# A search for best keys beside the compression of keys, and a sample group's last stages beside the experts' gathers

## The chip, the cores and the metric

One core of one Trainium2 chip runs the whole program. The metric is the device time of one execution in microseconds (us), lower is better. Three timed runs of the kernel before and one profiled execution are shown. PE is TensorE, DVE is VectorE, ACT is ScalarE, POOL is GpSimd, SP is SyncE, which here only issues DMAs.

## The reference

One layer of a decoder, for a prompt group (1 x 512 tokens, width 1024) and a sample group (8 sequences, one new token each, 4096 past tokens in paged caches of 128 rows). Both share all weights.

```python
xn = rmsnorm(x); p = xn @ w_in                       # one projection, columns split among the heads
# A: an indexer scores all keys, the best 256 are gathered, attention over them
# B: keys compressed by an MLP over strided chunks; the best 16 blocks of 64 tokens, gathered;
#    a window of 512; the three summed with gates
# M: attention into 256 memory tokens
u = einsum('btcw,cwd->btcd', stack([o_a, o_b, o_m]), w_branch)
h = x + sum(sigmoid(xn @ w_gate) * u, axis=2) @ w_out
q = rmsnorm(h) @ w_pq                                # 8 heads, each scored against 2 x 128 sub-keys
v_top, i_top = top_k(scores, 16); f_v, f_p = top_k(v_top[0] + v_top[1], 16)
g = softmax(f_v); e = the 16 experts of 16384
a = gelu(einsum('nhkd,nd->nhk', u_tab[e], xf))
y = h + einsum('nhk,nhkd->nd', g * a, v_tab[e])
```

For the sample group the compression reads all 256 pages of `cache_cmp_kv` (128 KB each), the search takes the best 256 of 4097 scores of each sample, and each of the 8 tokens draws 128 experts.

## The kernel before

Everything is float32. The program first projects, then does the prompt's attention, then the experts; the samples' attention lies beside the prompt's experts.

**The loop of gathers.** `mix_prompt` (line 3215) goes through 512 slots, 4 tiles of 128 tokens times 128 experts of each token. Slot n is one indirect DMA issued by POOL (line 3256): 128 rows of 8 KB, u and v of the expert side by side, into one of 7 buffers (`NBUF`). DVE multiplies u with the token's row and sums (line 3288), ACT makes the coefficient (gelu, times gate; lines 3316 and 3318). Three steps later (`LAG`) coefficient times v is added to y: either by DVE (line 3283), or by PE as a product with a diagonal matrix that ACT makes (lines 3323 and 3350). `adds_on_vector` says which; before, PE has steps 0 to 61, 175 to 238 and those of `SELECT`, DVE the rest. POOL issues slot s once slot s - 7 is summed and so free.

**Lanes beside the loop.** Each engine's program is in order. Work beside the loop is written as stages, each for a number of steps (`self.block(steps)`), and an engine's part yields fractions of its stage: `Beside.advance` puts the instructions up to step s ahead of the loop's instructions of step s. So a stage that waits on an engine holds the loop's instructions behind it. A stage begins, on every engine, with a wait until the lane's stage before has ended on all its engines. There are two lanes, `beside` and `aside`. SP has no part in the loop: it works through its own parts of the stages, in the order of steps but without being held to the loop's pace.

**Stages in order** (first step to last): retrieval of the prompt's later heads and tile 0 to 61; merge of gates, products, norm, products of the prompt's second half 62 to 174; retrieval of its tiles 175 to 238; weights of the compression 239 to 244; compression 245 to 316; index scores 317 to 344; queries 345; search for the best keys (`select_keys`) 346 to 381, with the window's attention and the memory's on the other lane from 348 and 354 on; attention over compressed keys 382 to 395; rows of the found keys 396 to 428; attention over them to 447; gather of chosen blocks 448 to 456; attention over blocks 457 to 496. The loop ends at step 519, after slot 511.

**Compression** (`compress_samples`, line 1253): 16 chunks of 16 pages, 3 buffers. For each page SP loads its number from a table and issues its DMA; chunk n is issued once PE has done chunk n - 3 (`part_mm`). PE does a chunk with 32 matmuls (line 1337), two chunks make a sample.

**Search** (`select_keys`, line 2294): 128 partitions hold 16 segments of each sample's scores. DVE does 32 rounds of max, max_index, match_replace (lines 2398 to 2400), then four levels of merging whose halves SP moves between partitions, then two short products.

**After the loop**, alone on the chip: `finish` calls `finish_rows` with `ahead=True` for the samples (merge of the branches, w_out, norm, w_pq; both weights are loaded during the merge), then `expert_samples`: the scores of 8 tokens, top 16, eight gathers of 1 MB, eight dot products, 32 matmuls, the store.

Of the kernel before, what the change touches and what calls it, by code (L numbers as in the profile page):

```python
# [8 lines left out]
F32 = mybir.dt.float32  # L9
U32 = mybir.dt.uint32  # L10
I32 = mybir.dt.int32
# [69 lines left out]
WEIGHTS, COMPRESS, INDEX, SELECT = 6, 72, 28, 36  # L81
WINDOW_FROM, WIN_AT, MEMORY, CMP_AT, DSA_AT, SEL_AT = 348, 16, 70, 14, 18, 40
DSA_ROWS = 30
# [144 lines left out]
class Kernel:  # L228
# [398 lines left out]
    def build(self):  # L627
        nc, i, o = self.nc, self.i, self.o
        with self.ctx:
# [17 lines left out]
            self.finish()  # L647
# [605 lines left out]
    def compress_samples(self, wts):  # L1253

        nc, i, ident = self.nc, self.i, self.ident
        tag = "cs"
# [3 lines left out]
        tmp = ExitStack()  # L1260
        with tmp:
            w2 = self.sb("cs_w2", [P, P], F32, tmp)
            table = self.sb("cs_table", [1, DB * NPAGE], I32, tmp)
            ch = self.sb("cs_ch", [P, NBUF, NPAGE // 2, 2, PAIRS, KV, 8], F32, tmp)
            part = self.sb("cs_part", [P, 2, 2, KV, NCH_S], F32, tmp)
# [5 lines left out]
            hp = self.ps("cs_hp", [P, 2, 512], tmp)  # L1271
            op = self.ps("cs_op", [P, 2, KV, 2, DH], tmp)
            kt = self.ps("cs_kt", [P, 512], tmp)
            (weights_in, table_in, zeroed, chain, part_mm, part_act, part_dve, hid_mm, hid_done, out_mm, out_v, kn_done, root_done, sq_sum,
             kt_mm, kt_out) = (self.sem(f"cs_{n}") for n in (
                 "weights_in", "table_in", "zeroed", "chain", "part_mm", "part_act", "part_dve", "hid_mm", "hid_done", "out_mm", "out_v",
# [9 lines left out]
            with self.block(WEIGHTS) as block:  # L1286
                @block.vector
                def _(dve):
                    dve.memset(w2[:], 0.0).then_inc(zeroed, 1)

                @block.sync
                def _(sp):
                    sp.dma_start(table[:], bass.AP(i["page_table"].tensor, 0, [[0, 1], [1, DB * NPAGE]])).then_inc(table_in, 16)
                    for c in range(2):
                        for j in range(2):
# [2277 lines left out]
```

## Time and profile before

| | |
|---|---|
| three runs, median | 2792.5 us (2788.6 to 2797.1) |
| the profiled execution | 2781.6 us, its span 2779.9 us |
| PE / DVE / ACT / POOL busy | 65% / 63% / 24% / 31% of the span |
| granted PE clock, mean | 0.787 of full |
| DMA | 727.7 MB, mean 262 GB/s; the gathers' queue 577 MB |

The chain that ended last names only the last 2% of the span, so the profile has to be read by stages: busy time of each engine, PE clock and DMA share in the stretch of each stage, and in it who waits for whom. "DMA share" is the mean busy share of the sixteen DMA engines.

### The profile page before, as it was taken

What the parts mean: (1) busy time and instruction counts of PE and PEld (TensorE: products, weight loads), DVE (VectorE), ACT (ScalarE), POOL (GpSimd) and SP (SyncE); (2) the same over time, 40 slices, a digit from 0 to 9 for tenths busy, and PEclk for the clock granted to TensorE, in tenths of its full rate; (3) what the DMA queues carried; (4) which work ended last, traced back from release to release, by engine and by line L of the source; (5) the groups of instructions that cost most, each with busy time, mean ns of one, the idle gap of its engine ahead of it and who ended that gap; (6) DMA issues with size and microseconds to landing.
All of it is one profiled execution on the core that took longest, in us unless ns stands there. A gap on an engine that the chain in (4) does not pass through costs nothing. (4 is left out here: it accounts for less than half of the span.)

```text
span 2779.9 us, 25050 instructions
## 1 busy us (share of the span) xinstructions
PE 1812.3 (65%) x6605; PEld 1000.1 (36%) x6605; DVE 1761.6 (63%) x3916; ACT 670.4 (24%) x2035; POOL 864.9 (31%) x829
## 2 busy tenths in 40 slices
PE   7999799699836738844467515665877533418374
PEld 3466476444412213312222114444743213304311
DVE  3343465711168967685789965666779688859813
ACT  2011266410113323321233211222222111214100
POOL 1000042200024723342353432221531477654301
PEclk9999799899969969977799957878568755555586
DMA  4122320043248989997998898996986799899863
GB/s 150 25 88 76 96 92 2 1 166 130 104 167 349 421 348 358 355 392 306 377 379 326 356 367 311 350 355 246 404 343 247 295 351 374 324 363 398 330 227 122
DMA packets 200920, 727.69 MB, mean 262 GB/s; under 512 B 39785, under 2 KB 83330, under 8 KB 133898
## 3 DMA queue, kind: packets, MB, share of 16 engines
q0 software_dynamic: 84384, 577.16, 52.0%
q1 hardware_dynamic: 115226, 144.70, 15.3%
q10 hardware_dynamic: 1168, 4.23, 0.4%
q8 instruction: 54, 0.88, 0.1%
q14 instruction: 88, 0.72, 0.1%
HBM read 717.42 MB, written 12.66 MB: 263 GB/s over the span
## 5 line engine op out<-in xcount | busy, mean ns | idle before, releaser
L3256 POOL DMA_INDIRECT ex_pairs<-in_uv_tab,e_idx x147 | 196.0, 1333 | 552.9 <-POOLq L3153 246.7
L3316 ACT ACTIVATE ex_coef<-ex_dots 128x1 f32<-128x1 f32 x512 | 103.6, 202 | 1046.8 <-DVE ex_dots L3288 953.9
L3256 POOL DMA_INDIRECT branch_rows_t<-in_uv_tab,e_idx x163 | 192.2, 1179 | 256.8 <-DVE heads_t L3283 160.4
L3256 POOL DMA_INDIRECT heads_t<-in_uv_tab,e_idx x146 | 186.0, 1274 | 268.4 <-DVE heads_t L3283 146.8
L1337 PE MATMUL cs_pp<-cs_ch,xn_t 128*128 128x256 f32 x512 | 146.3, 456 | 175.9 <-DMA cs_ch<-in_cache_cmp_kv 175.9
L3288 DVE CUSTOM_DVE_ANT_0 branch_rows_t<-branch_rows_t,heads_t 128x1024 f32<-128x1024 f32 x163 | 198.6, 1220 | 55.2 <-DMA branch_rows_t<-in_uv_tab,e_idx 50.3
L3288 DVE CUSTOM_DVE_ANT_0 ex_pairs<-ex_pairs,heads_t 128x1024 f32<-128x1024 f32 x147 | 179.5, 1222 | 60.9 <-DMA ex_pairs<-in_uv_tab,e_idx 58.9
L820 PE MATMUL in_acc<-in_w,xn_t 128*128 128x512 f32 (+7 forms) x560 | 208.1, 527 | 5.8 <-POOLq L178 4.0
L3288 DVE CUSTOM_DVE_ANT_0 heads_t<-heads_t 128x1024 f32<-128x1024 f32 x146 | 178.1, 1221 | 37.8 <-DMA heads_t<-in_uv_tab,e_idx 34.9
L1337 PEld LDWEIGHTS cs_pp<-cs_ch,xn_t 128*128 128x128 f32 x512 | 118.5, 235 | 205.9 <-DMA cs_ch<-in_cache_cmp_kv 106.8
L3283 DVE SCALAR_TENSOR_TENSOR heads_t<-branch_rows_t,ex_coef,heads_t 128x1024 f32<-128x1024 f32 x118 | 151.2, 1281 | 30.6 <-issue 14.7
L3318 ACT ACTIVATE ex_coef<-ex_coef,e_gate 128x1 f32<-128x1 f32 x512 | 150.8, 295 | 16.6
L3350 PE MATMUL ex_y_ps<-ex_pairs,heads_t 128*128 128x512 f32 x188 | 98.9, 657 | 76.9 <-ACT heads_t L3323 71.8
L3283 DVE SCALAR_TENSOR_TENSOR heads_t<-ex_pairs,ex_coef,heads_t 128x1024 f32<-128x1024 f32 x100 | 127.9, 1279 | 28.5 <-issue 24.9
L3283 DVE SCALAR_TENSOR_TENSOR heads_t<-heads_t,ex_coef 128x1024 f32<-128x1024 f32 x100 | 128.0, 1280 | 25.5 <-issue 22.2
L820 PEld LDWEIGHTS in_acc<-in_w,xn_t 128*128 128x128 f32 (+1 forms) x560 | 95.1, 174 | 108.3 <-issue 88.4
L3350 PE MATMUL ex_y_ps<-heads_t 128*128 128x512 f32 x184 | 99.0, 667 | 47.8 <-ACT heads_t L3323 38.6
L3350 PE MATMUL ex_y_ps<-branch_rows_t,heads_t 128*128 128x512 f32 x180 | 96.2, 666 | 31.8 <-ACT heads_t L3323 30.9
L1638 PE MATMUL at_t_ps<-at_diag,at_exp 128*128 128x128 f32 (+3 forms) x608 | 87.6, 288 | 21.7 <-POOL at_diag L1726 20.9
L2925 PE MATMUL fq_mg_g_ps<-fq_mg_wg,xn_t 128*128 128x512 f32 x192 | 85.0, 596 | 0.0
L3350 PEld LDWEIGHTS ex_y_ps<-ex_pairs,heads_t 128*128 128x128 f32 x188 | 35.6, 205 | 135.5 <-ACT heads_t L3323 97.8
L1638 PEld LDWEIGHTS at_t_ps<-at_diag,at_exp 128*128 128x128 f32 (+3 forms) x608 | 71.9, 185 | 34.6 <-POOL at_diag L1726 22.0
(727 smaller groups left out, 3435.1 us busy)
## 6 DMA issues: line engine op xcount, KB each, us to landing
cs_ch<-in_cache_cmp_kv SPq DMA_DIRECT2D x256, 128.0 KB
fq_mg_wg<-in_w_gate SPq DMA_DIRECT2D x6, 2048.0 KB
in_w<-in_w_in SPq DMA_DIRECT2D x4, 2048.0 KB, 11.3
first_w<-in_w_gate SPq DMA_DIRECT2D x3, 2048.0 KB, 7.9
fp_wb<-in_w_branch SPq DMA_DIRECT2D x6, 1024.0 KB, 10.2
fp_wg<-in_w_gate SPq DMA_DIRECT2D x3, 2048.0 KB, 8.1
fq_mg_wb<-in_w_branch SPq DMA_DIRECT2D x6, 1024.0 KB
fs_mg_wb<-in_w_branch SPq DMA_DIRECT2D x6, 1024.0 KB, 9.8
```

Of the source, the lines that this page charges most:

```text
L820: last = pe.matmul(acc[:r, u % 2, :n], self.xT[:, k, P * t:P * t + r], w[:, j % 2, k, :n], start=(k == 0), stop=(k == KD - 1))
L1337: last = pe.matmul(pp[:, n % 2, 256 * c:256 * c + 256].rearrange("p (g k m) -> p g k m", g=KV, m=8), wts[:, c, r, :], ch[:, n % NBUF, :, c ...
L1638: last = pe.matmul(t_ps[:w, u % 2, k, :], ex[:, u % 6, P * k:P * k + w], diag[:, u % 4, :], start=True, stop=True)
L2925: last = pe.matmul(g_ps[:r, u % 2, :], xT[:, k, cols], wg[j % depth][:, k, :], start=(k == 0), stop=(k == KD - 1))
L3256: pool.indirect_dma_start(out=pair(s), out_offset=None, in_=i["uv_tab"], in_offset=bass.IndirectOffsetOnAxis(ap=idx[:, t, m:m + 1], axis=0 ...
L3283: dve.scalar_tensor_tensor(out=y(t), in0=v(n), scalar=coef[:, t, m:m + 1], in1=y(t), op0=ALU.mult, op1=ALU.add).then_inc(acc_done, 1)
L3288: dve.tensor_tensor_reduce(out=u(s), in0=u(s), in1=x(t), scale=1.0, scalar=0.0, op0=ALU.mult, op1=ALU.add, accum_out=dots[:, t, m:m + 1]). ...
L3316: act.activation(c, dots[:, t, m:m + 1], ACT.Gelu_apprx_tanh).then_inc(gelu_done, 1)
L3318: act.activation(c, c, ACT.Copy, scale=gate[:, t, m:m + 1]).then_inc(coef_done, 1)
L3350: last = pe.matmul(y_ps[:, q, :], diag[:, (pe_upto[n] - 1) % NDIAG], v(n)[:, 512 * q:512 * q + 512], start=n in first_pe, stop=n in last_pe)
```

## The change

The search for best keys moves to the second lane and runs beside the compression, which now stands behind the index scores; the compression's weights are loaded in one step ahead of the index. The samples' merge, products, norm and experts become stages beside the gathers, at the end of the lane; w_out and w_pq are now loaded by their own stages. The loop's sums from step 267 on alternate, even slots on DVE and odd ones on PE. New steps: weights 239, index 240 to 267, compression 268 to 339, beside it the search 268 to 317, the picks 318 to 333, their places 334 to 336; queries 340; window 341 to 362 and memory 363 to 422 on the second lane; compressed keys' attention 341 to 354, found rows 341 to 370, attention over them to 389, gather of blocks 390 to 397, attention over blocks 399 to 442; merge 443 to 452, turn, w_out 456 to 465, norm, w_pq 472 to 481, turn, experts of the samples 485 to 519. Some buffers change place (the window's values, the search's lists, two banks of PSUM become one).

```diff
-WEIGHTS, COMPRESS, INDEX, SELECT = 6, 72, 28, 36
-WINDOW_FROM, WIN_AT, MEMORY, CMP_AT, DSA_AT, SEL_AT = 348, 16, 70, 14, 18, 40
+INDEX, COMPRESS, SELECT, PICKED = 28, 72, 50, 16
+WIN_AT, MEMORY, CMP_AT, DSA_ROWS, DSA_AT, SEL_AT = 16, 60, 14, 30, 18, 44
+LAST_MERGE, LAST_TURN, LAST_LINEAR, LAST_NORM, LAST_ROWS = 10, 3, 10, 6, 34
+GATHERED, MIXED = 10, 28
...
-    picking = retrieving + RETRIEVE_LAST + WEIGHTS + COMPRESS + INDEX
-    return not (step < RETRIEVE_HALF + RETRIEVE_NEXT or retrieving <= step < retrieving + RETRIEVE_LAST or picking <= step < picking + SELECT)
+    indexing = retrieving + RETRIEVE_LAST
+    if step < RETRIEVE_HALF + RETRIEVE_NEXT or retrieving <= step < indexing:
+        return False
+    return step < indexing + INDEX or m % 2 == 0
...
             with self.block(COMPRESS) as block:
                 @block.sync
                 def _(sp):
+                    sp.wait_ge(table_in, 16)
                     for n in range(2 * DB):
                         if n >= NBUF:
+                            yield at((n - NBUF) // 2, 0.1 + 0.5 * ((n - NBUF) % 2))
                             sp.wait_ge(part_mm, n - NBUF + 1)
...
-                        if u >= 2:
-                            pe.wait_ge(hid_done, u - 1)
+                        if u:
+                            pe.wait_ge(hid_done, u)
...
     def sample_attention(self):
...
+                weights = self.sample_compress_weights(tmp, wts)
+                self.index_scores()
+                self.recycle()
+                indexed = main.before
+                self.aside.next_step = main.next_step
+                self.compress_samples(tmp, wts, weights, part)
+                self.beside = self.aside
+                with ExitStack() as sk:
+                    chosen = self.select_keys(sk, [(main.ended, indexed)])
+                    self.aside.next_step += PICKED
+                    self.place_keys(chosen, phys, past_ix, is_new)
...
             with self.block(SELECT) as block:
                 @block.sync
                 def _(sp):
+                    for sem, value in ready:
+                        sp.wait_ge(sem, value)
                     sp.dma_start(work[:, :W], bass.AP(s["score"].tensor, 0, [[W, NSEG], [PAST, DB], [1, W]])).then_inc(work_in, 16)
...
                         for n in range(LEVELS):
                             half = P >> (n + 1)
+                            yield 0.61 + 0.2 * n / LEVELS
                             sp.wait_ge(merged, n + 1)
...
+            work = ExitStack()
+            with work:
+                self.finish(work, keys)
...
-            with nc.Block() as block:
+            remembered = self.aside.ended, self.aside.before
+            with self.block(LAST_MERGE) as block:
                 @block.sync
                 def _(sp):
-                    sp.dma_start(gate8[:], self.s["gate8"].rearrange("j b n -> b j n")).then_inc(gate_in, 16)
                     for j, (q, c) in enumerate(jobs):
                         sp.dma_start(wb[:, j], i["w_branch"][c, :, 512 * q:512 * q + 512].rearrange("(k p) n -> p k n", p=P)).then_inc(w_in[j], 16)
                     for dst, src in also:
                         sp.dma_start(dst, src).then_inc(also_done, 16)
-                    for dst, src, loaded in ahead:
-                        sp.dma_start(dst, src).then_inc(loaded, 16)
+                    sp.wait_ge(*remembered)
+                    sp.dma_start(gate8, self.s["gate8"].rearrange("j b n -> b j n")).then_inc(gate_in, 16)
...
             @block.sync
             def _(sp):
-                beside.advance("sync", sp, 10 ** 9)
+                for s in list(range(end)) + [10 ** 9]:
+                    beside.advance("sync", sp, s)
+                    aside.advance("sync", sp, s)
...
+            with self.block(LAST_ROWS) as block:
                 @block.gpsimd
                 def _(pool):
                     pool.memset(q[:], 0.0).then_inc(zeroed, 1)
-                    pool.wait_ge(idx_done, 2)
                     for n in range(N):
-                        pool.indirect_dma_start(out=pairs[:, n], out_offset=None, in_=i["uv_tab"],
+                        yield at(GATHERED + 0.8 * n)
+                        if n == 0:
+                            pool.wait_ge(idx_done, 2)
+                        pool.indirect_dma_start(out=pairs[n], out_offset=None, in_=i["uv_tab"],
```

## Rows read from the trace of the kernel before

**Rows 1.** The page's slices of the span, 40 of 69.5 us each
```profile
DMA  4122320043248989997998898996986799899863
GB/s 150 25 88 76 96 92 2 1 166 130 104 167 349 421 348 358 355 392 306 377 379 326 356 367 311 350 355 246 404 343 247 295 351 374 324 363 398 330 227 122
```

**Rows 2.** Timeline of DVE; start, duration, line; steps 239 and 511
```profile
1599.55 1.22 DVE L3288 CUSTOM_DVE_ANT_0 ex_pairs<-ex_pairs,heads_t 128x1024 f32<-128x1024 f32 x1
...
2632.85 1.23 DVE L3288 CUSTOM_DVE_ANT_0 ex_pairs<-ex_pairs,heads_t 128x1024 f32<-128x1024 f32 x1
```

**Rows 3.** Busy us by stage: stretch, length, PE, PEld, DVE, ACT, POOL, clock, DMA, GB/s
```profile
1600.00:1613.00 13.00, 0.00 (x0) 0.00 (x0) 12.95 (x19) 2.88 (x12) 6.77 (x6) 0.50 1.11 354
1613.00:1956.00 343.00, 177.00 (x676) 137.70 (x676) 208.18 (x365) 67.15 (x195) 97.01 (x79) 0.74 0.88 326
1956.00:2052.00 96.00, 83.32 (x373) 78.19 (x373) 84.52 (x150) 22.34 (x74) 42.26 (x36) 0.52 0.92 376
2052.00:2214.00 162.00, 108.27 (x286) 46.48 (x286) 119.27 (x349) 35.04 (x111) 47.96 (x53) 0.84 0.73 287
2214.00:2374.00 160.00, 47.29 (x183) 35.84 (x183) 129.93 (x212) 30.07 (x103) 121.07 (x108) 0.53 0.95 367
2374.00:2488.00 114.00, 33.19 (x128) 22.80 (x127) 71.33 (x104) 20.48 (x76) 67.80 (x58) 0.50 0.84 328
2488.00:2600.00 112.00, 95.75 (x336) 60.03 (x336) 103.09 (x139) 38.21 (x148) 49.65 (x40) 0.50 0.97 391
2600.00:2634.00 34.00, 0.00 (x0) 0.00 (x0) 33.89 (x45) 6.97 (x28) 12.38 (x11) 0.50 0.92 367
2634.00:2780.00 146.00, 80.10 (x204) 22.09 (x204) 37.73 (x89) 10.90 (x27) 9.88 (x9) 0.75 0.45 167
...
805.00:2634.00 1829.00, 1045.43 (x3131) 575.39 (x3131) 1389.97 (x2748) 462.50 (x1435) 767.93 (x629) 0.73 0.89 349
```

**Rows 4.** Waits in the compression: total us, times, longest
```profile
PE cs_pp L1337 <- DMA cs_ch<-in_cache_cmp_kv: 175.9, 15, 76.5
```

**Rows 5.** Timeline of SP: start, us, issues; pages 0 to 47, then 48 to 255
```profile
1609.90 72.38 SPq L1314 DMA_DIRECT2D cs_ch<-in_cache_cmp_kv  x48
...
1683.08 238.84 SPq L1314 DMA_DIRECT2D cs_ch<-in_cache_cmp_kv  x208
```

**Rows 6.** Timeline of PE: two chunks that follow each other
```profile
1801.86 8.58 PE L1337 MATMUL cs_pp<-cs_ch,xn_t 128*128 128x256 f32 x32 [6.54 <-DMA cs_ch<-in_cache_cmp_kv]
...
1817.74 9.17 PE L1337 MATMUL cs_pp<-cs_ch,xn_t 128*128 128x256 f32 x32 [6.41 <-DMA cs_ch<-in_cache_cmp_kv]
```

**Rows 7.** Timeline of SP: the scores stored, then loaded for the search
```profile
2045.86 0.39 SPq L2211 DMA_DIRECT2D tmp_score<-is_score  x1
2051.83 0.61 SPq L2342 DMA_DIRECT2D sk_work<-tmp_score  x1
```

**Rows 8.** Groups of DVE in the search, 2052 to 2214: busy us, mean ns, idle before
```profile
L2398 DVE MAX8 sk_best<-sk_work 128x8 f32<-128x257 f32 x32 | 13.6, 425 | 0.4
L2399 DVE FIND_INDEX8 sk_ix<-sk_best,sk_work 128x8 uint32<-128x257 f32 x32 | 13.4, 420 | 0.0
L2400 DVE MATCH_REPLACE8 sk_work<-sk_best,sk_work 128x257 f32<-128x257 f32 x32 | 13.2, 412 | 0.0
```

**Rows 9.** The page's group of sums on DVE: busy us, mean ns, idle before
```profile
L3283 DVE SCALAR_TENSOR_TENSOR heads_t<-branch_rows_t,ex_coef,heads_t 128x1024 f32<-128x1024 f32 x118 | 151.2, 1281 | 30.6 <-issue 14.7
```

**Rows 10.** Timeline of PE: one sum, its four matmuls, in the index stage
```profile
2043.82 3.58 PE L3350 MATMUL ex_y_ps<-branch_rows_t,heads_t 128*128 128x512 f32 x4 [0.26 <-issue]
```

**Rows 11.** Largest group of PE at 1406 to 1600
```profile
L3350 PE MATMUL ex_y_ps<-branch_rows_t,heads_t 128*128 128x512 f32 x79 | 39.6, 629 | 11.1 <-ACT heads_t L3323 10.9 <-issue 0.2
```

**Rows 12.** Timeline of the tail: first gather, its first use, the last matmuls
```profile
2735.15 0.95 POOL L3403 DMA_INDIRECT es_pairs<-in_uv_tab,es_idx  x1 [16.73 <-DVE es_idx L3483]
...
2740.98 1.23 DVE L3492 CUSTOM_DVE_ANT_0 es_pairs<-es_pairs,es_xf 128x1024 f32<-128x1024 f32 x1 [4.62 <-DMA es_pairs<-in_uv_tab,es_idx]
...
2760.99 15.32 PE L3422 MATMUL es_y_ps<-es_pairs,es_diag 128*8 128x512 f32 x32 [32.59 <-ACT es_diag L3438]
```

More of the change, by code:

```diff
@@ new lines, in sample_dsa @@
+            prob = self.sb("cm_prob", [DB * HQ, NCH_S + DB], F32, ctx)
+            compressed = self.beside.ended, self.beside.before
+            queries = self.spread_queries(qz, qa, placed)
+            compared = []
+            windowed = self.sample_window(ctx, qz, nsa, queries, compressed, compared)
+            self.sample_memory(bank, queries)
+            rows_at = self.beside.next_step
+            landed = self.gather("da_rows", [(kv[:, n // DB, n % DB, :], i["cache_a_kv"].rearrange("n p w -> (n p) w"), phys[:, n:n + 1]) for n in range(2 * DB)]
+                                 + [(bias[:, n // DB, n % DB, :], s["bias_pos"], past_ix[:, n:n + 1]) for n in range(2 * DB)], apart=True, steps=DSA_ROWS,
+                                 behind=placed)
@@ new lines, in sample_dsa @@
+            self.attend_samples("cm_at", NCMP_S, HQ, qz, keys=lambda b: self.kc_t[:, b, :NCMP_S],
+                                values=lambda b, j: self.vc[:min(P, NCMP_S - P * j), b, j].rearrange("p g d -> p (g d)"), acc=nsa, turned=False,
+                                waits=lambda b: [queries], bias=self.bias_cmp, prob=prob, gate=self.gate_bh[:, 0:1], add=False, steps=CMP_AT, scoring=0.3)
+            compared.append((self.beside.ended, self.beside.before))
+            self.pick_blocks(prob, sl_rows, sl_bias_rows)
@@ L2456, in select_keys @@
             rows = s["cand"].rearrange("p (k w) -> (p k) w", w=1)
-            picked = self.gather("sk_pick", [(t_f[:, n:n + 1], rows, cand_at[:, n:n + 1]) for n in range(NC)], apart=True, steps=16)
+            picked = self.gather("sk_pick", [(t_f[:, n:n + 1], rows, cand_at[:, n:n + 1]) for n in range(NC)], apart=True, steps=PICKED)
             return picked, t_f, t_i, page, hot
@@ L2727, in finish_rows @@
             out_w = pq_w = None
-            loads = []
-            if ahead:
-                out_w, pq_w = ((self.sb(f"{tag}_{n}_early", [P, 2, KD, 512], F32, tmp)[:], [self.sem(f"{tag}_{n}_early{b}") for b in range(2)])
-                               for n in ("out", "pq"))
-                loads = [(w[:, b], i[name][:, 512 * b:512 * b + 512].rearrange("(k p) n -> p k n", p=P), sems[b])
-                         for name, (w, sems) in (("w_out", out_w), ("w_pq", pq_w)) for b in range(2)]
             weights, after, then = None, [], []
@@ L2767, in finish_rows @@
             turn("mixed", t_view, load_h)
-            self.linear(f"{tag}_out", t_view, rows, i["w_out"], D, h, add=h, loaded=out_w, ahead=then)
-            if not ahead and not early:
+            self.linear(f"{tag}_out", t_view, rows, i["w_out"], D, h, add=h, loaded=out_w, ahead=then, steps=linear_steps)
+            if not early:
                 self.recycle()
-            self.norm_rows(f"{tag}_ffn", h, i["ln_ffn"], rows, t_view, keep=xf)
-            self.linear(f"{tag}_pq", t_view, rows, i["w_pq"], D, mixed, also=[(save, h)] if save is not None else (), loaded=pq_w)
+            self.norm_rows(f"{tag}_ffn", h, i["ln_ffn"], rows, t_view, keep=xf, steps=norm_steps)
+            self.linear(f"{tag}_pq", t_view, rows, i["w_pq"], D, mixed, also=[(save, h)] if save is not None else (), loaded=pq_w, steps=linear_steps)
             turn("pq", x_t)
```

309 lines of the change are left out of this document (168 added, 141 removed).

## The prediction

> **What bounds the kernel now.** I read the page first: its slices [rows 1] show that from about 800 us on the sixteen DMA engines are eight to nine tenths busy, and that the last slices fall off. That is the loop of 512 gathers (1 MB each, one a step). Its first dot product starts at 812 us; the n-th execution of line 3288 on VectorE is step n, and with that the stages can be laid on the clock: step 239 is at 1599.6 us and step 511, the last, at 2632.9 us [rows 2]. Then I read one window per stage [rows 3]. The reader is to see three kinds. In most of them the DMA share is 0.92 to 0.97 (there the transfers are the limit, 367 to 391 GB/s). In two it is lower though all engines have room: the compression (343 us for 72 steps, 4.8 us a step, share 0.88) and the search for best keys (162 us for 36 steps, share 0.73). And the last 146 us, where the samples' own merge, products, retrieval and experts run alone, have a share of 0.45, 66 us of DMA work in 146.
>
> Inside the compression, TensorE waits 175.9 us in 15 waits for the pages of the cache [rows 4]. Pages are issued by SP, one instruction chain each: 208 of them take 238.8 us without a hole, 1.15 us a page or 18.4 us for the 16 pages of one chunk [rows 5], and TensorE starts chunks 16 to 18 us apart, though one takes it 8.6 to 9.2 us [rows 6]. So SP's issuing sets the pace of that stage.
>
> **A rule weighed.** The Trainium skill ("DMA: Bandwidth & Descriptors", Issuing engines are not separate DMA queues) says that the sequencer's time to start a DMA is usually small beside the transfer. By that rule the stage would be priced by its bytes. The trace doesn't agree: 208 issues stand back to back over 238.8 us while TensorE waits [rows 4, 5]; what the rule would make of the time is the first rival.
>
> **The change, part by part**, each step range with its time before and after. Steps 0 to 238 are not touched: 1599.6 us stay.
>
> Index (steps 239 to 267): the weights' stage shrinks from 6 steps to 1, index keeps 28. Before, 28 steps took about 96 us [rows 3]; with one more step 100 us.
>
> Compression with the search beside it (steps 268 to 339). Both start at once, and SP serves both in the order of steps: it first issues 48 pages, and only then the table of scores that VectorE's search needs at step 271. 48 pages took 72 us when the gathers competed [rows 5]; at 1.15 us each 55. VectorE, and with it the gathers, stands still meanwhile; I take 58 us, near the undisturbed rate since the gathers stop too, and 6 us more for the scores to land (the hand-over of the same data took 6 us from store to next load [rows 7]). That is a new wait, and behind it on VectorE stand all dot products. Then some 18 us until TensorE has done chunk 0 and SP may issue the fourth. The other 208 pages take 239 us. The search's own DMAs on SP hold pages back: four exchanges of lists and two round trips for the bar; the trace has no such wait beside pages, so from 0 (TensorE's three chunks of stock cover it) to six times 6 us; I take 12. After its last page the stage took 35 us more (1921.9 to 1956). Sum 58 + 6 + 18 + 239 + 12 + 35 = 368, say 370 us (330 to 400), for 343 before. The search on VectorE costs 13.6 + 13.4 + 13.2 us in its three large groups [rows 8], 40 us, and some 70 (an estimate) with the levels of merging behind them; VectorE was busy 208 of 343 us [rows 3] and gives 36 sums of 1.28 us [rows 9] to TensorE, so 208 - 46 + 70 = 232 us of 370: hidden, until VectorE's idle time, some 140 us, is gone. What was 162 us of its own for the search is gone.
>
> Steps 340 to 370 (window, compressed keys' attention, picked blocks, gathers of rows): 47 such steps took 160 us [rows 3], 3.4 a step, so 31 take 105; the window's 4.2 MB, which lay in the search before, add 11 at 367 GB/s: 116 us (105 to 130).
>
> Steps 371 to 398 (the attention over chosen keys, gather of blocks): 28 steps took 114 us; 3 us more for memory rows: 117.
>
> Steps 399 to 442 (attention over blocks): 2.8 us a step [rows 3], 44 steps 123 us, and 3.4 MB of memory rows 9: 132 us. Here the alternation weighs: a sum on TensorE, four matmuls, took 3.6 us at the lower level of its clock [rows 10] and 2.0 us (79 matmuls in 39.6 us) in a stage where sums filled it [rows 11]; and TensorE was already busy 95.8 of 112 us with the clock at 0.50. 22 sums more are 44 to 79 us, on 96 x 44/40 = 105 us: 149 us at the cheaper price of a sum and 184 at the dearer; the attention's own matmuls would also take about half if the clock rose for them, which would leave the 123 us of the gathers as the limit. I take 145 (123 to 184), near the first of these, since the clock was 0.84 in the one stage where sums and attention shared TensorE (2052 to 2214).
>
> The Trainium skill ("TensorE: Matmul & The Clock Gate", What's actually happening) has the clock released by activity. The trace only half agrees: 0.84 at 108 of 162 us busy, but 0.50 at 96 of 112 [rows 3]. By the page this part would cost 132; I don't rely on it.
>
> Samples' finish beside gathers (steps 443 to 510). Bytes: 68 gathers are 71 MB, the weights 6.3 + 4.2 + 4.2, the samples' eight gathers 8.4, gain and small 0.5: 95 MB. At the best window's 391 GB/s 243 us, at the 328 of the stretch with most hand-overs (2374 to 2488) 290. The chain now loads w_out and w_pq in their own stages (they were loaded ahead), so TensorE waits for them with sums queued behind it; POOL, up to seven gathers ahead, waits at step 485 for the turned rows and at 495 for the indices, and one gather needs 5.8 us from issue to the first use [rows 12]. I take 265 us, midway. VectorE's and TensorE's own work of the tail (38 and 80 us [rows 3]) is spread over it.
>
> End (from step 511): seven steps of sums, the eight diagonals, 32 matmuls in 15.3 us [rows 12], the addition and store, 7 + 2 + 15 + 3 = 27 us (to 40), in place of the 147 us from 2632.9 to 2779.9.
>
> **Sum.** 100 + 370 + 116 + 117 + 145 + 265 + 27 = 1140 us in place of 1180; the execution ends at 1599.6 + 1140 = 2739.6, and with the 1.7 us that lie between span 2779.9 and time 2781.6 that is 2741. The median of the runs, 2792.5, is 10.9 above the profiled one, which makes 2752, rounded: I forecast **2750 us** as median, 1.5% faster. A cross-check: DMA busy time from step 239 on is the sum of share times length over rows 3, 976 us; the forecast gives it 1113 us outside the end, a share of 0.88, which is what the loop has now (0.89).
>
> **Rivals.** First, SP's issuing is no limit and the freed VectorE lets the gathers run at 0.95, the share of the better windows: 976 / 0.95 = 1027, plus 27 is 1054 in place of 1140, so about 2665 us. For it speaks that the tail is idle at 0.45 and that VectorE loses 110 us of work (122 sums on TensorE from step 267 on in place of 36, 86 x 1.28); against it the unbroken issues [rows 5]. This is also what the page named above would give.
>
> Second, slower: **TensorE becomes the bound at half clock**. With sums on every second step it has gaps and stays at 1.2 GHz: 3.6 us every two steps. Attention over blocks goes to 184 (+39); the finish, where TensorE has the tail's 80 us of matmuls [rows 3] at the mixed clock of 0.75 and 34 sums of 3.6, gets +25, as a chain through slower matmuls (80 x 0.75 / 0.5 = 120, +40, of which part is covered); the compression +10: 2750 + 74 = 2824. It decides once work per step on TensorE, 2.4 us of attention and 1.8 of sums, passes the 2.8 us of a gather. For it: a clock of 0.50 to 0.53 in all windows from 2214 to 2634. Against: 0.84 where every sum ran on TensorE.
>
> Third, no change: the first wait of the search costs the full 72 us and the finish comes at 290: 2750 + 14 + 12 for SP's exchanges + 25 = 2801 at most, 2790 typical; the tail's gain is spent on new waits.
>
> **Chances.** Forecast 0.56 (2690 to 2780), first rival 0.21, second 0.12, third 0.11. A measurement can tell about 0.3% from none, 8 us: faster than 2784 holds the forecast and the first rival, 0.77; within 0.11; slower 0.12. The range 2665 to 2805 leaves out the faster half of the first rival and most of the second.
>
> **What would show it.** After: dot product 268 near 1700 us, then a hole of 50 to 70 us in them with SP issuing 48 pages; step 340 near 2070; TensorE's waits for pages still near 150 us; no stretch with only the search; sums on TensorE in every second step, at a clock of 0.6 to 0.8; last dot product near 2710; end 27 us later. The prediction is wrong if the compression with the search takes under 330 or over 400 us, if the finish takes over 4.3 us a step, or if attention over blocks takes over 4 us a step with TensorE full.

## The result, and the profile after

The kernel after takes 2808.9 us (median of 11 runs, 2799.0 to 2820.9), the kernel before in the same comparison 2786.9 us (11 runs, 2780.5 to 2797.2). The ratio is 1.0076 with a 95% interval of 1.0054 to 1.0098: **slower by 0.8%**, where 2750 us and faster was forecast, and above the top of the range, 2805. The profiled execution of after took 2820.9 us (the highest of its runs), its span is 2817.5 us. It moves 727.66 MB, before 727.69.

The page's slices, to be laid beside [rows 1] (40 of 70.4 us each; DMA is the busy share in tenths, GB/s what was moved):

```profile
DMA  4122310054158989897998797796869898887776
GB/s 148 25 93 71 115 69 2 1 180 163 53 230 355 400 339 373 347 395 303 363 376 331 271 416 268 280 368 234 299 244 376 346 370 342 315 315 275 305 320 254
```

Most of the drop in before's last slices (227 and 122 GB/s) is gone, as intended. In its place stand 268 and 280 from 1690 us on, 234 and 244 between 1900 and 2110, and nothing above 320 in the last six slices. The windows by stage (stretch, length, busy us of PE, PEld, DVE, ACT and POOL with instructions, granted clock, DMA share, GB/s), beside [rows 3]:

```profile
1606.00:1624.00 18.00, 3.65 (x16) 3.28 (x16) 3.16 (x7) 1.08 (x3) 10.37 (x10) 0.50 0.96 274
1624.00:1722.00 98.00, 85.26 (x380) 77.31 (x380) 83.76 (x146) 22.34 (x74) 44.21 (x42) 0.53 0.91 368
1722.00:1778.00 56.00, 3.78 (x4) 1.18 (x4) 7.89 (x14) 1.89 (x7) 3.03 (x3) 0.54 0.63 221
1778.00:1886.00 108.00, 83.68 (x291) 53.11 (x292) 103.62 (x267) 28.03 (x85) 32.05 (x29) 0.86 0.95 355
1886.00:2006.00 120.00, 70.81 (x239) 44.89 (x238) 61.92 (x167) 22.20 (x63) 20.79 (x20) 0.72 0.70 246
...
2344.00:2503.00 159.00, 147.24 (x532) 90.48 (x533) 87.32 (x130) 47.71 (x178) 52.93 (x46) 0.74 0.82 311
2503.00:2556.00 53.00, 39.59 (x77) 9.03 (x76) 24.07 (x35) 6.98 (x25) 12.30 (x11) 0.86 0.87 321
2556.00:2696.00 140.00, 72.72 (x175) 25.96 (x175) 62.59 (x93) 26.99 (x90) 37.42 (x34) 0.75 0.76 295
2696.00:2792.00 96.00, 45.16 (x64) 14.75 (x62) 62.48 (x119) 22.31 (x72) 31.80 (x31) 0.66 0.89 367
2792.00:2818.00 26.00, 17.97 (x37) 3.97 (x36) 7.62 (x13) 2.75 (x12) 0.00 (x0) 0.83 0.06 22
805.00:2792.00 1987.00, 1267.70 (x3639) 629.82 (x3639) 1318.38 (x2736) 504.19 (x1536) 742.14 (x638) 0.78 0.86 333
```

Four stretches are to be seen. At 1722 to 1778 (steps 268 to 270) and 1886 to 2006 (steps 300 to 317) no engine is full (at most 71 of 120 us in the second) and the DMA share is 0.63 and 0.70: somebody waits. At 2344 to 2503 (attention over blocks) PE is busy 147 of 159 us: it is the bound. At 2556 to 2696 (from the samples' turn and w_out on) the share is 0.76 and again no engine is full.

With the n-th dot product as the mark of step n, as in the prediction, the miss in the profiled execution, 77.9 us on 2739.6, falls into these parts. It is larger than the 59 us by which the medians miss, since this execution is 12 us above the median of its kernel, and the profiled one of before was below its own:

| steps | forecast us | after us | miss |
|---|---|---|---|
| start to 239 | 1599.6 | 1606.1 | +6.5 |
| 239 to 268, index | 100 | 116.3 | +16.3 |
| 268 to 340, compression and search | 370 | 384.2 | +14.2 |
| 340 to 371 | 116 | 121.0 | +5.0 |
| 371 to 399 | 117 | 116.4 | -0.6 |
| 399 to 443, attention over blocks | 145 | 158.8 | +13.8 |
| 443 to 511, samples' finish | 265 | 289.4 | +24.4 |
| end | 27 | 25.2 | -1.8 |

Steps 0 to 238 run the same work; their 6.5 us are the spread of executions (1593 to 1609 in the kernels below). Part of the 14.2 us is spread too: four kernels below with the same code in steps 268 to 339 (e4, e7, e8, e12) take 369.0 to 378.3 us for them.

**The waits of the search.** SP's timeline (start, us, line, what, count) at step 268, and the wait of DVE at step 270:

```profile
1716.92 55.30 SPq L1319 DMA_DIRECT2D cs_ch<-in_cache_cmp_kv  x48
1772.26 0.60 SPq L2367 DMA_DIRECT2D sk_work<-tmp_score  x1
```
```profile
DVE sk_best L2429 <- DMA sk_work<-new_key_score: 45.3, 1, 45.3
```

It is the forecast hole: 48 pages before the table of scores, 1.15 us a page. SP's timeline from there to the end of its pages, and DVE's waits in 1886 to 2006:

```profile
1791.78 109.80 SPq L1319 DMA_DIRECT2D cs_ch<-in_cache_cmp_kv  x96
1901.62 0.55 SPq L2376 DMA_DIRECT2D sk_moved<-sk_best  x1
...
1903.57 17.21 SPq L1319 DMA_DIRECT2D cs_ch<-in_cache_cmp_kv  x16
1920.82 8.17 SPq L2376 DMA_DIRECT2D sk_moved<-sk_over  x2
1929.79 16.81 SPq L1319 DMA_DIRECT2D cs_ch<-in_cache_cmp_kv  x16
1946.65 0.73 SPq L2376 DMA_DIRECT2D sk_moved<-sk_over  x1
1958.30 17.24 SPq L1319 DMA_DIRECT2D cs_ch<-in_cache_cmp_kv  x16
1975.59 0.37 SPq L2382 DMA_DIRECT2D tmp_bar<-sk_bar  x1
1978.46 0.62 SPq L2384 DMA_DIRECT2D sk_bar<-tmp_bar  x1
1980.48 93.56 SPq L1319 DMA_DIRECT2D cs_ch<-in_cache_cmp_kv  x64
```
```profile
DVE sk_over L2458 <- DMA sk_bar<-tmp_bar: 16.8, 1, 16.8
DVE sk_over L2441 <- DMA sk_moved<-sk_best: 16.7, 1, 16.7
...
DVE sk_over L2441 <- DMA sk_moved<-sk_over: 12.9, 2, 10.8
```

An exchange of lists that DVE needs at once stands in SP's order behind pages that nobody needs yet, the first behind the end of a run of 96, later ones behind a chunk of 16, 17 us. DVE waits 46.4 us for them, and behind it on DVE stand all dot products. I had looked at it from the other side only: what the exchanges do to the pages. TensorE waited for pages 11.7 us and not some 150 (the page's group of its matmuls; idle before in the last column):

```profile
L1344 PE MATMUL cs_pp<-cs_ch,xn_t 128*128 128x256 f32 x512 | 118.1, 390 | 11.7 <-DMA cs_ch<-in_cache_cmp_kv 11.7
```

**The waits of the finish**, 2503 to 2792 us (total, times, longest):

```profile
PE fs_pq_acc L488 <- DMA fs_pq_w<-in_w_pq: 21.5, 1, 21.5
DVE fs_mixed L3038 <- DMA xn_t<-tmp_gate: 21.1, 1, 21.1
...
PE fs_out_acc L488 <- DMA fs_out_w<-in_w_out: 18.6, 1, 18.6
```

PE waits in full for each of the two weights that were loaded ahead before, and the merge for its gates, whose load stands on SP behind the 6 MB of w_branch: these took SP 24.5 us to issue (2502.27 to 2526.78), the gates' load followed at 2529.17, and the merge could begin at 2539.7.

### The profile page after: what moved, and what is told of

It reads as the page before. It is cut to its first block and busy times, and to the rows that moved or that the text cites. A ratio compares the mean times of both kernels' runs of the same rounds, so it can differ in the third digit from the quotient of the medians.

```text
span 2817.5 us, 25696 instructions
## 1 busy us (share of the span) xinstructions
PE 1972.8 (70%) x6945; PEld 1035.6 (37%) x6945; DVE 1660.0 (59%) x3831; ACT 703.6 (25%) x2121; POOL 828.7 (29%) x829
## 2 busy tenths in 40 slices
DMA packets 200778, 727.66 MB, mean 258 GB/s; under 512 B 39769, under 2 KB 83186, under 8 KB 133754
## 5 line engine op out<-in xcount | busy, mean ns | idle before, releaser
L3382 PE MATMUL ex_y_ps<-branch_rows_t,heads_t 128*128 128x512 f32 x324 | 196.1, 739 | 144.9 <-ACT heads_t L3355 129.6
L3382 PE MATMUL ex_y_ps<-ex_pairs,heads_t 128*128 128x512 f32 x288 | 171.4, 728 | 93.2 <-ACT heads_t L3355 91.7
L3382 PE MATMUL ex_y_ps<-heads_t 128*128 128x512 f32 x280 | 160.7, 705 | 55.3 <-ACT heads_t L3355 54.8
L3382 PEld LDWEIGHTS ex_y_ps<-branch_rows_t,heads_t 128*128 128x128 f32 x324 | 67.5, 227 | 241.3 <-ACT heads_t L3355 149.0
L3382 PEld LDWEIGHTS ex_y_ps<-ex_pairs,heads_t 128*128 128x128 f32 x288 | 60.5, 228 | 183.7 <-ACT heads_t L3355 124.7
L1344 PE MATMUL cs_pp<-cs_ch,xn_t 128*128 128x256 f32 x512 | 118.1, 390 | 11.7 <-DMA cs_ch<-in_cache_cmp_kv 11.7
L3315 DVE SCALAR_TENSOR_TENSOR heads_t<-branch_rows_t,ex_coef,heads_t 128x1024 f32<-128x1024 f32 x82 | 105.0, 1281 | 28.1 <-issue 16.6
L3315 DVE SCALAR_TENSOR_TENSOR heads_t<-ex_pairs,ex_coef,heads_t 128x1024 f32<-128x1024 f32 x75 | 96.0, 1280 | 26.9 <-issue 24.1
L3382 PEld LDWEIGHTS ex_y_ps<-heads_t 128*128 128x128 f32 x280 | 55.6, 215 | 140.1 <-ACT heads_t L3355 87.8
L3315 DVE SCALAR_TENSOR_TENSOR heads_t<-heads_t,ex_coef 128x1024 f32<-128x1024 f32 x76 | 97.3, 1280 | 11.0 <-DMA fs_ffn_gain<-in_ln_ffn 4.0
## 6 DMA issues: line engine op xcount, KB each, us to landing
in_w<-in_w_in SPq DMA_DIRECT2D x4, 2048.0 KB, 11.3
fs_mg_wb<-in_w_branch SPq DMA_DIRECT2D x6, 1024.0 KB, 25.2
```

The source lines that it names most:

```text
L1344: last = pe.matmul(pp[:, n % 2, 256 * c:256 * c + 256].rearrange("p (g k m) -> p g k m", g=KV, m=8), wts[:, c, r, :], ch[:, n % NBUF, :, c ...
L3315: dve.scalar_tensor_tensor(out=y(t), in0=v(n), scalar=coef[:, t, m:m + 1], in1=y(t), op0=ALU.mult, op1=ALU.add).then_inc(acc_done, 1)
L3382: last = pe.matmul(y_ps[:, q, :], diag[:, (pe_upto[n] - 1) % NDIAG], v(n)[:, 512 * q:512 * q + 512], start=n in first_pe, stop=n in last_pe)
```

## The experiments

The ratios are to the kernel before, in parentheses the 95% interval, with the median of the changed kernel. Every kernel is the one after with the edit shown, unless it says otherwise; each computes the whole output. The theory: waits in SP's order of issue and late weights cost the time (A). The rival: sums on PE do (B). Others are named in the expectations.

**e1: Sums back on DVE.**

```diff
-    return step < indexing + INDEX or m % 2 == 0
+    return True
```

> The changed kernel with all sums from step 267 on made by VectorE again (only the alternation is undone). Theory A (the loss sits in waits on SP's queue: 55 us at step 271 and about 46 us at the exchanges of the search) expects little: attention over blocks falls from 159 to some 130 us as TensorE, busy 147 of 159, is relieved, the compression with the search grows by some 15 as VectorE takes 36 sums of 1.28 us back: 2790 to 2805 us for 2809. Rival B (TensorE is the bound of the late stages through its sums) expects 30 us less in attention over blocks and 20 to 30 in the samples' finish: 2750 to 2760 us.

Measured 1.0103 (1.0068 to 1.0138), 2820.7 us: far from B's 2750 to 2760, and above A's 2790 to 2805 too. That it is slower than after (1.0076) the intervals do not tell. The rows of steps 399 to 442 and of 271 to 299:

```profile
2371.00:2507.00 136.00, 119.80 (x448) 83.90 (x448) 112.00 (x152) 39.83 (x156) 54.33 (x47) 0.50 0.95 368
1780.00:1906.00 126.00, 42.42 (x172) 29.82 (x172) 121.46 (x282) 22.71 (x72) 33.91 (x29) 0.65 0.92 319
```

Attention over blocks falls from 158.8 to 135.8 us and is bound by the transfers again (share 0.95 for 0.82). But in the rounds of the search DVE is now full, 121 of 126 us, and steps 271 to 299 take 127 for 108. The finish takes 297.4 us for 289.4. The alternation helps in one place and costs in another; as the cause of the whole, B falls.

**e2: Scores ahead of the pages.** SP loads the table of scores before the first 48 pages.

```diff
                     sp.wait_ge(table_in, 16)
+                    yield 0.02
                     for n in range(2 * DB):
```

> The changed kernel, but SP loads the table of scores for the search ahead of the first 48 pages instead of behind them. Theory A: the hole of 55 us before dot product 271 falls to about 12, and most of it is time won, as the pages were not late afterwards (TensorE waited 12 us for them in all): 2765 to 2775 us. Rival D (SP's issuing of 256 pages, 1.15 us each, sets the length of the stage whatever stands still in it) expects the time back as waits for pages: 2800 to 2810 us.

Measured 1.0063 (1.0036 to 1.0089), 2806.6 us: from 1.0076 no difference that can be told. A had expected 2765 to 2775, D 2800 to 2810. The hole did go: steps 268 to 270 take 10.2 us for 55.2. But SP still has to issue the same pages, now 144 of them in 177 us without a hole, and TensorE waits for them, 42.7 us for 11.7. Steps 271 to 299 take 28 us more and 300 to 317 take 12 more. SP's first run of pages, and TensorE's wait in 1720 to 2100:

```profile
1710.58 177.03 SPq L1320 DMA_DIRECT2D cs_ch<-in_cache_cmp_kv  x144
...
PE cs_pp L1345 <- DMA cs_ch<-in_cache_cmp_kv: 42.7, 5, 17.9
```

Of 45 us, 40 were spent again by step 318. The hole had given SP a head start; without it SP's rate of issue shows. (Over all of steps 268 to 339 the profiled execution takes 365.7 us, 18.5 less than after but only 3 to 13 less than the four kernels with unchanged code there, and the medians lie 2.3 us apart: what stays of it is not told by these runs.)

**e3: Pages apart.** SP issues pages one by one as the steps go, so that an exchange finds a place between them.

```diff
                         for k in range(NPAGE // 2):
+                            if n >= NBUF:
+                                yield at((n - NBUF) // 2, 0.1 + 0.5 * ((n - NBUF) % 2) + 0.03 * k)
```

> The changed kernel, but SP's pages of one chunk are spread over the four steps of that chunk in its order of work, so that the search's exchanges of lists and its bar don't stand behind 16 pages (17 us) each. Theory A: VectorE's waits of 16.7, 12.9 and 16.8 us at the exchanges fall to some 3 each, and 30 to 40 us are won: 2770 to 2780 us. Rival D: pages then wait behind the search instead, TensorE's waits for pages grow by the same: 2800 to 2815 us.

Measured 1.0017 (0.9992 to 1.0043), 2794.1 us: 0.6% faster than after. Steps 300 to 317 take 95.3 us for 119.8 (117.0 to 119.8 in the kernels with unchanged code there), and that is all of the gain up to step 340. SP's timeline in them, and their window:

```profile
1896.33 13.55 SPq L1321 DMA_DIRECT2D cs_ch<-in_cache_cmp_kv  x13
1909.93 0.53 SPq L2378 DMA_DIRECT2D sk_moved<-sk_over  x1
1911.58 8.05 SPq L1321 DMA_DIRECT2D cs_ch<-in_cache_cmp_kv  x8
1921.71 0.74 SPq L2378 DMA_DIRECT2D sk_moved<-sk_over  x1
```
```profile
1875.00:1970.00 95.00, 67.72 (x238) 43.11 (x237) 61.40 (x166) 21.92 (x61) 20.55 (x21) 0.82 0.84 294
```

The work in the window is the same (DVE 61 us in both), the waits behind 16 pages are not there: DVE waits 3.0 us for the later exchanges and 2.7 for the bar, where it waited 12.9 and 16.8. D had expected TensorE's wait for pages to grow, and it stayed at 11.3 us. So A is shown for these. The wait at step 300, for the first exchange, stays (14.2 us for 16.7).

**e5: Both orders together.**

> Both edits of SP's order at once: scores loaded ahead of the pages, and pages spread over their chunk's steps. The scores first gave 4 us and the spread pages 16 us (ratios 1.0063 and 1.0017 for 1.0076). If SP's queue is one resource, the hole at step 271 is paid back only because pages come late later; with the exchanges out of the way too, the two add up at most: ratio 1.000 to before (theory A). If both only shift the same wait, the ratio stays at 1.0017 (rival D).

Measured 0.9992 (0.9966 to 1.0017), 2787.9 us: 0.84% under after, where the two alone gave 0.13 and 0.59%. Whether the first edit adds anything once the second is in these runs don't tell: 0.25% lies between e3 and e5, as much as either interval reaches to one side. In the profiled execution the first hole is gone again (10.4 us for steps 268 to 270), and DVE's wait for the first exchange has grown to 26.7 us.

**e4: The finish alone at the end again**, with everything else as after: the call of `finish` moves behind the loop.

> The changed kernel with the samples' merge, products, retrieval and experts after the loop again, all else as changed (w_out and w_pq are not loaded ahead). Theory A: beside the gathers they take 290 us for 68 steps and 25 at the end; alone the 68 steps are bare at 2.5 us, 170 us, and the tail takes the 147 of before and some 25 more for weights that are not loaded ahead: 342 for 315, so 2830 to 2840 us. Rival C (hand-overs between lanes eat what the overlap gives): 2800 us or less.

Measured 1.0150 (1.0119 to 1.0180), 2830.1 us. In A's range. Steps 443 to 510 take 172.3 us and the end 164.9, together 337.2; after, 289.4 + 25.2 = 314.6. So the finish beside the gathers is a gain of 0.7% even with its waits. And the rest of the change is a loss, in two places. With the finish alone, dot product 511 comes at 2653 us and not at 2633, though the search's own stage is gone: the window and the memory, which lay beside that search [rows 3, 2052 to 2214], now lie beside later steps, and the compression with the search takes 369 us here for 72 steps where before it took 343 alone. And the end takes 165 us where before, with w_out and w_pq loaded ahead, it took 147.

**e6: The kernel before with the alternation** from the search on (all even slots on DVE, odd on PE; nothing else changed).

```diff
+    if step >= picking:
+        return m % 2 == 0
```

> The kernel before with only the alternation: from the search on, even slots' sums on VectorE and odd ones' on TensorE (in the search TensorE had all, later VectorE all; the compression keeps VectorE). In the changed kernel undoing the alternation cost 0.3%, a gain of 34 us elsewhere and a loss of 23 us in attention over blocks. The kernel before has no samples' finish beside the gathers, where it could gain: I expect 20 us lost in attention over blocks and 10 won in the search: ratio 1.000 to 1.005. A ratio under 0.997 would say that the alternation is a gain by itself.

Measured 1.017 (1.011 to 1.023), 2832.6 us. The stage of the search takes 180.8 us for 155.1 (DVE had no sums there before; now it has half of them), attention over blocks 128.9 for 111.7:

```profile
2511.00:2640.00 129.00, 119.79 (x411) 71.43 (x412) 79.12 (x118) 45.06 (x168) 41.69 (x39) 0.76 0.85 333
```

I had expected 10 us won in the search, and 26 were lost. In the order of before, alternating is a loss of its own, 1.7%; 9 us of it lie in steps 245 to 316, which the edit does not touch (352.0 us for 342.7), and stay unexplained. Which engine has room depends on what lies beside the step.

**e8: Alternation everywhere but in the attention over blocks.**

```diff
-    return step < indexing + INDEX or m % 2 == 0
+    return step < indexing + INDEX or 399 <= step < 443 or m % 2 == 0
```

> The changed kernel with sums on VectorE in steps 399 to 442 alone, the alternation kept elsewhere. With all sums on VectorE these steps took 136 us for 159. If TensorE (147 us busy of 159) is the bound there, 20 to 23 us are won: ratio 1.000 (rival B, for these steps alone). If it only moves waits, ratio 1.005 to 1.008.

Measured 0.9983 (0.9952 to 1.0013), 2786.5 us, 0.9% under after. The stage takes 135.8 us for 158.8:

```profile
2335.00:2471.00 136.00, 121.58 (x450) 84.73 (x451) 112.29 (x152) 40.36 (x157) 54.95 (x47) 0.50 0.96 368
```

Here B is right: with 82 matmuls fewer the transfers bound the stage again. What the sums cost on TensorE, from its groups in 2344 to 2503 of after, and the memory's products in 2335 to 2471 of e8 (busy us, mean ns, idle before):

```profile
L3382 PE MATMUL ex_y_ps<-branch_rows_t,heads_t 128*128 128x512 f32 x36 | 26.7, 882 | 0.3 <-issue 0.3
L3382 PE MATMUL ex_y_ps<-heads_t 128*128 128x512 f32 x24 | 16.8, 837 | 0.3 <-issue 0.3
L3382 PE MATMUL ex_y_ps<-ex_pairs,heads_t 128*128 128x512 f32 x24 | 16.3, 815 | 1.2 <-ACT heads_t L3355 1.2
...
L2721 PE MATMUL me_ps<-values,xn_t 128*128 128x1 f32 x112 | 25.0, 353 | 0.0
```

84 matmuls are 21 sums in 59.8 us, 2.85 us a sum. The rest of TensorE's 147.2 us, 87 us, is attention with the memory's products, which took 119.5 us in e8 at the lower level of the clock.

**e7: The finish's weights ahead.** Three of the four halves of w_out and w_pq go into the merge's buffers as its products leave them, during the merge, and the fourth behind w_out's products; the norm gets scratch that is free by then.

```diff
+                loads = [(2, places[0], half("w_out", 0), sems[0]), (4, places[1], half("w_out", 1), sems[1]), (6, places[2], half("w_pq", 0), sems[2])]
+                then = [(nt, places[0], half("w_pq", 1), sems[3])]
...
                     sp.dma_start(gate8, self.s["gate8"].rearrange("j b n -> b j n")).then_inc(gate_in, 16)
+                    for count, dst, src, loaded in loads:
+                        sp.wait_ge(branch_mm, count)
+                        sp.dma_start(dst, src).then_inc(loaded, 16)
```

> The changed kernel, but w_out and w_pq are loaded into the merge's own buffers as these come free, ahead of their stages. TensorE waited 19 and 22 us for them, with odd sums queued behind it, and each of these two stages took 51 us for 10 steps where 10 bare steps take 25. If the waits are the cause (theory A), each falls to about 36 us: 25 to 30 us won, ratio 0.998. If the stages are limited by their bytes, 14.7 MB in 51 us being 288 GB/s (rival E), under 8 us are won: ratio 1.005.

Measured 0.9962 (0.9935 to 0.9988), 2774.5 us, 1.1% under after and now faster than before. The two stages take 33.3 us for 51.7 and 28.4 for 50.8; steps 443 to 510 take 255.0 for 289.4. The bytes are the same, and TensorE's two waits for weights are gone (the merge still waits 21.8 us for its gates); the window over both stages (2530 to 2628) against 0.76 and 295 GB/s in after:

```profile
2530.00:2628.00 98.00, 68.98 (x148) 21.87 (x146) 62.51 (x89) 26.45 (x88) 34.05 (x31) 0.80 0.95 380
```

**e10: All four edits together.**

> The four edits that each won something, together: scores loaded first, pages spread, w_out and w_pq loaded ahead, sums on VectorE in steps 399 to 442. They lie in different steps (268 to 339, 456 to 481, 399 to 442), so theory A and B together expect the gains to add: 0.84 + 1.14 + 0.93 = 2.9% under the changed kernel's 1.0076, ratio 0.979, about 2730 us. If the transfers of the whole loop are the real limit (rival E), the gains overlap and the ratio stays at 0.99.

Measured 0.9772 (0.9737 to 0.9807), **2724.5 us** (six runs, 2716.2 to 2732.8): 2.3% faster than before, 3.0% faster than after. The parts alone (e5, e8, e7) sum to 0.84 + 0.93 + 1.14 = 2.9%: they add up, so they were separate costs. Its loop, to be read beside the last window row of after (0.86, 333 GB/s) and of [rows 3] (0.89, 349):

```profile
805.00:2700.00 1895.00, 1251.30 (x3550) 635.52 (x3551) 1343.22 (x2758) 495.23 (x1513) 745.65 (x637) 0.76 0.89 349
```

**e11: The same with all sums of steps 268 to 317 on PE.**

```diff
+    if 268 <= step < 318:
+        return False
```

> The same with all sums of steps 268 to 317 on TensorE, as the kernel before had them beside its search. Alternating them in the kernel before made its 36 steps of search 26 us longer, as VectorE has search, dot products and sums. Beside the compression TensorE has the chunks too (118 us busy for them). If VectorE is the bound there: 10 to 20 us less than e10_all; if TensorE with pages is: 10 us more.

Measured 0.9784 (0.9740 to 0.9828), 2725.2 us: no difference. Neither the 10 to 20 us less nor the 10 more of the expectation came. In 1717 to 2070 DVE is busy 207 of 353 us, TensorE 262, and the DMA share is 0.85 (0.84 in the same stage of e10). With the orders mended, neither engine bounds the compression. What is left is SP: in e10 issuing its 256 pages takes it 315 us beside a stage of 355. That is an account from the timeline; no run made the issuing itself cheaper.

**e12: The compression's weights on the second lane**, to see whether SP's issues make the 18 us of step 239.

```diff
-                weights = self.sample_compress_weights(tmp, wts)
+                self.beside, self.aside.next_step = self.aside, main.next_step
+                weights = self.sample_compress_weights(tmp, wts, (main.ended, main.before))
+                self.beside = main
+                main.next_step += 1
...
```

> The changed kernel with the compression's weights loaded in a stage of the second lane, so that the index scores don't wait until SP has issued their seven DMAs. Step 239 took 18 us for some 3; if the seven issues (5.5 us) stand in it, it takes 12 us or less. If the hole is POOL's (it goes up to seven gathers ahead and waits for the stage's begin, then the first four index gathers stand ahead of the next dot product's), it stays at 15 to 18.

One execution, 2822.1 us; step 239 takes 22.7 us, neither the 12 of one account nor the 15 to 18 of the other. The start of the index stage in after:

```profile
1610.41 0.94 POOL L2244 DMA_INDIRECT is_ch<-in_cache_a_kidx,chunk_rows  x1 [30.17 <-SPq L180]
...
1613.96 1.28 DVE L3315 SCALAR_TENSOR_TENSOR heads_t<-branch_rows_t,ex_coef,heads_t 128x1024 f32<-128x1024 f32 x1 [3.13 <-DMA is_w<-tmp_w]
...
1616.37 0.94 POOL L3288 DMA_INDIRECT heads_t<-in_uv_tab,e_idx  x1 [0.30 <-issue]
...
1624.14 1.22 DVE L3320 CUSTOM_DVE_ANT_0 heads_t<-heads_t 128x1024 f32<-128x1024 f32 x1 [8.89 <-DMA heads_t<-in_uv_tab,e_idx]
```

In before (first two lines) and in e12 (last line):

```profile
1943.34 0.94 POOL L2221 DMA_INDIRECT is_ch<-in_cache_a_kidx,chunk_rows  x1 [31.68 <-DVEq L177]
...
1948.31 0.94 POOL L3256 DMA_INDIRECT heads_t<-in_uv_tab,e_idx  x1 [0.30 <-issue]
...
1625.15 1.28 DVE L3320 SCALAR_TENSOR_TENSOR heads_t<-branch_rows_t,ex_coef,heads_t 128x1024 f32<-128x1024 f32 x1 [19.78 <-DMA is_w<-tmp_w]
```

POOL reaches the start of the index stage seven gathers ahead and stands there 24 to 32 us, until the stage before has ended; then it issues the index's own gathers, and only 5 to 6 us later one of the loop. In after DVE's 18.0 us between dot products 239 and 240 hold three waits: 2.9 us until SP has issued the seven loads, 3.1 for `is_w`, the index scores' weights, whose load follows on SP, and 8.9 for the loop's gather. In e12 POOL was released 6 us earlier against the loop's steps and issued the loop's next gather at 1607.33, but DVE stood 19.8 us for `is_w` (by the profile), still issued behind the seven loads. So the edit moved a wait and took none away, and what each of the three costs alone stays open. The kernel before has such a hole too: its dot product 316 is at 1934.8 us and 317 at 1956.5. I had read "28 steps in 96 us" from a window that begins at 1956.

## Why the prediction was wrong, point by point

**What bounds it.** The reading of before held: SP's issuing sets the compression's pace (in e2, once the hole is gone, 144 pages are issued in 177 us without a pause while TensorE waits for them), the tail left the DMA engines idle, and attention over blocks is bound by transfers as long as PE has no sums (135.8 us in four kernels, 132 worked out). The list of stretches with a low share left out one of its own rows, 2374 to 2488 with 0.84, but the sums used it.

**Index, 100 for 116.** A term taken from a window that starts behind the hole at the stage's first step. A hole of this kind came along with the stage: step 239 alone takes 18.0 us.

**Compression and search, 370 for 384.** The first hole was right: 55.2 us for steps 268 to 270. Wrong was the next term, 12 us for SP's exchanges: I priced the wait of the pages for the exchanges (6 us each at most, hidden by three chunks), and put the wait of DVE for an exchange behind pages at nothing; it was 46 us in sum. Since pages are issued 1.15 us apart [rows 5], 16 of them are 18 us, and each DMA in the same order can wait that long; the rows for it were there. Followed along SP, as the forecast was added up, the stage comes out as 50 us from dot product 268 to the end of the first 48 pages (58 forecast), 20 until the next page (24), 255 for the other 208 pages (239), 28 in pauses between runs of pages at the exchanges (12) and 33 after the last page (35). By the code SP waits in these pauses for DVE's lists and TensorE's chunks, and both stand behind DVE's waits; in e3 the pauses are 15 us and the stage 361. TensorE's waits for pages, 12 us instead of some 150, were wrong too: while DVE and with it the chunks stood still, SP got ahead.

**Attention over blocks, 145 for 159.** The step that failed is TensorE's own sum of work. A sum was taken near its cheaper end, 2.0 us, and took 2.85, between that and 3.6. And the attention's work was put at 96 x 44/40 = 105 us: the stage's work does not grow with its number of steps, while the memory's products beside it, 25 us at the lower level (112 matmuls in e8), counted only as bytes; e8 has 119.5 us in all. The clock did rise, to a mean of 0.74, and made these 87 us, but with 60 us of sums TensorE still needed 147. The upper half of the range of 123 to 184 held it. The second rival had named this stage; its clock did not stay at 0.50, and of the three places it named, the compression (e11: no difference with more sums on PE) and the finish (e1: 297 us with all sums on DVE, for 289) showed no such cost. Its outcome, slower, came with a chance of 0.12, and mostly by other ways than its own.

The Trainium skill's rule on clock release by activity ("TensorE: Matmul & The Clock Gate", What's actually happening) agreed in part: the mean clock was 0.74 here, between its two levels. But in 2464 to 2484 TensorE was busy all of 20 us and the clock was at its lower level, 0.50, and 132 us, which I had worked out by the page, did not come.

**Finish, 265 for 289.** The mechanism was named (TensorE waits for w_out and w_pq with sums queued behind), but it had no term of its own: I took the middle of two transfer rates. The waits measured 21.5, 18.6 and, for the gates, 21.1 us; e7 takes 34 us out of the stretch and lands at 255, under the forecast. The gates' wait it leaves as it is.

**End, 27 for 25**, and steps 340 to 398, 233 for 237: right.

**The first rival** (SP no limit, share 0.95) fell: the best kernel's loop has 0.89. The rule of the Trainium skill that stood beside it ("DMA: Bandwidth & Descriptors", Issuing engines are not separate DMA queues), that starting a DMA is usually small beside the transfer, doesn't hold for these pages of 128 KB. Issuing 48 of them, 6.3 MB, took 55.3 us again, and at the 367 GB/s of the better windows their bytes take 17 (an estimate).

**The third rival** (no change, the tail's gain spent on new waits, at most 2801) was the nearest, short by 8 us of the median. Of its three terms the finish at 290 came (289.4), the exchanges cost 16 us more than forecast (28 for 12) where it had 12 more, and the full 72 us for the first hole did not come (55). Its list lacked the hole at the index's start and the second rival's stage. I had kept second and third apart, as if only one could come; both came in part, and their misses had one sign.

**The signs named beforehand** did not catch this. Dot product 268 came at 1722 us (near 1700), the hole was 55 us (50 to 70), step 340 came at 2107 (near 2070) and the last dot product at 2792 (near 2710). But none of the three bounds was passed: the compression took 384 us (330 to 400), the finish 4.26 us a step (4.3), attention over blocks 3.6 (4). Each of these parts was inside its bound, and the sum was outside its range.

**Open.** DVE still waits 14.2 us (e3) to 30.0 us (e11) for the search's first exchange at step 300, more where the first hole is gone; SP is issuing pages without a pause until then (138 in 171 us in e10), which no run tried to mend. Nor did any run mend the gates' wait. That the hole at the index's start could be closed by issuing gathers of the loop first was not tried either.

## What to carry to other kernels

When a stage moves beside another one, list for every engine that issues for both what stands ahead of each of its short, urgent DMAs at that point: behind a batch of 16 loads each one can cost the whole batch, 17 us here, and a latency that was nothing when the stage ran alone becomes a stand of the main loop. A weight that was loaded ahead must stay ahead after the move: here the two waits cost 34 of the 56 us that the move could bring (337 us with the finish alone, 281 with the weights ahead). And where work alternates between two engines, choose by stage: the same alternation was worth 18 us in the search's rounds and cost 23 in the attention over blocks.

## What was unexpected of the hardware

That more work on TensorE went with a higher granted clock where it was already nearly full. In the attention over blocks without sums TensorE was busy 121.6 of 136 us (e8) and the clock was 0.50, the level of 1.2 GHz, all the way. With half of the loop's sums beside it the mean clock was 0.74 (after) and 0.76 (e6). It was not the same all through; two stretches of 20 us of after, in both of which TensorE was full:

```profile
2364.00:2384.00 20.00, 20.00 (x85) 11.41 (x83) 8.95 (x13) 6.49 (x28) 7.66 (x8) 0.83 0.86 319
2464.00:2484.00 20.00, 20.00 (x68) 15.64 (x68) 7.36 (x12) 3.69 (x13) 6.34 (x5) 0.50 0.71 267
```

In the second, 59 of the 68 matmuls are the attention's last products (line 2027) and the other nine belong to the loop's sums. So in these rows neither busy time nor the presence of sums tells the level, and no run separates which work does. The higher clock didn't pay: it took the attention and the memory's products from 119.5 to 87 us, the sums added 60, and the stage took 159 us for 136.
